# Mixer in a new order, LayerNorm by token half, band matrices from the host: one change to a hybrid decoder kernel

## The reference

```python
u = rms_norm(h, norm_mix_g)
b_a, c_a, h_a, v_b, g_b = split(u @ w_in)                 # five parts of 512 channels
y_a = b_a * causal_dwconv(c_a * h_a, conv_a_w)            # 3 taps
cb  = causal_dwconv(v_b * sigmoid(g_b), conv_b_w) + bias  # 31 taps
y_b = silu(layer_norm(cb, ln_b_g, ln_b_b))                # over 512 channels
h   = h + concat(y_a, y_b) @ w_out
h   = h + cross_attention(rms_norm(h), rms_norm(mem))     # 4 heads
h   = h + relu(rms_norm(h) @ w_up) ** 2 @ w_down          # width 4096
# after both layers: rms_norm(h, final_g)
```

## Time and profile before

| | us |
|---|---|
| median of 3 runs | 3471.89 (3469.18 to 3646.47) |
| the profiled execution | 3468.78 |
| its span, slowest core | 3467.2 |
| spans of all cores | 3442.4 to 3467.2 |
| TensorE busy | 3257.5 (94%) |
| VectorE / ACT / POOL busy | 1762.9 / 1402.1 / 643.7 |

### The profile page before, as it was taken

One profiled execution on the slowest core, in us unless ns is written; L12 is line 12 of the kernel. 1 busy time (PEld: TensorE's weight loads), 2 busy tenths in 40 slices (PEclk: granted clock), 3 DMA queues, 4 the chain that ended last, 5 costly groups with the idle time before them and its releaser, 6 DMA issues.

```text
span 3467.2 us, 50455 instructions; the slowest of 8 cores (3442.4 to 3467.2 us)
## 1 busy us (share of the span) xinstructions
PE 3257.5 (94%) x16080; PEld 1550.2 (45%) x16080; DVE 1762.9 (51%) x2912; ACT 1402.1 (40%) x2627; POOL 643.7 (19%) x884
## 2 busy tenths in 40 slices
PE   2879999999998999989998999999999899999997
PEld 0445444444454444544444444444445444454443
DVE  4846333663357532564347743376335753366433
ACT  3336322463325531464333732256333553146421
POOL 0413001320032100330004200222003210042000
PEclk9989999999999999999999999999999999999999
DMA  7686944544555444535548344344456444453441
GB/s 202 150 187 102 166 73 85 118 91 79 110 167 124 80 78 82 122 79 86 98 94 228 64 80 76 91 113 83 77 117 177 111 80 79 75 127 72 77 80 52
DMA packets 132275, 366.93 MB, mean 106 GB/s; under 512 B 13872, under 2 KB 39728, under 8 KB 132016
## 3 DMA queue, kind: packets, MB, share of 16 engines
q0 software_dynamic: 59648, 213.94, 36.5%
q1 hardware_dynamic: 63152, 145.56, 13.3%
q10 hardware_dynamic: 9216, 4.20, 0.5%
HBM read 521.98 MB, written 34.60 MB: 161 GB/s over the span
## 4 chain that ended last, share of the span: by engine, by line
PE 83%; DVE 4%; issue 4%; DMA 3%; ACT 3%; POOL 1%; SPq 1%; DVEq 0%; ACTq 0%; POOLq 0%
PE ps L450 81%; ACT arena L461 3%; DMA arena<-wts 2%; DVE arena L465 2%; PE ps L906 2%; DVE arena L475 1%; DMA wbf<-arena 1%; SPq L577 1%; POOL arena L465 1%; DVE arena L610 0%; POOL arena L479 0%; POOL arena L470 0%; POOL arena L766 0%; DVE arena L951 0%; SPq L589 0%
## 5 line engine op out<-in xcount | busy, mean ns | idle before, releaser
L450 PE MATMUL ps<-arena 128*128 128x512 bf16 (+2 forms) x15816 | 3182.7, 364 | 126.3 <-ACT arena L461 64.9
L450 PEld LDWEIGHTS ps<-arena 128*128 128x128 bf16 x15816 | 1520.8, 98 | 1785.8 <-issue 175.6
L461 ACT ACTIVATE arena<-arena 128x512 bf16<-128x512 f32 (+3 forms) x1249 | 740.6, 642 | 1265.2 <-DVE arena L465 949.3
L465 DVE TENSOR_TENSOR arena<-arena 128x512 bf16<-128x512 f32 (+3 forms) x1200 | 849.5, 715 | 653.6 <-ACT arena L461 632.2
L465 DVE TENSOR_TENSOR arena<-ps,arena 128x512 f32<-128x512 f32 (+1 forms) x448 | 303.2, 688 | 633.7 <-PE ps L450 594.4
L461 ACT ACTIVATE arena<-ps 128x512 f32<-128x512 f32 (+1 forms) x608 | 361.8, 595 | 623.0 <-PE ps L450 599.2
L416 POOL DMA_DIRECT2D arena<-wts x400 | 214.7, 538 | 1662.6 <-PE ps L450 1621.1
L465 POOL TENSOR_TENSOR arena<-arena 128x512 f32<-128x512 f32 (+1 forms) x144 | 206.7, 1439 | 609.3 <-ACT arena L461 366.0
L461 ACT ACTIVATE arena<-ps,arena 128x256 f32<-128x256 f32 (+2 forms) x441 | 228.6, 533 | 135.9 <-DVE arena L471 72.9
L465 DVE TENSOR_TENSOR arena<-arena,ps 128x512 f32<-128x512 f32 x256 | 172.8, 686 | 141.2 <-PE ps L906 81.6
L475 DVE SCALAR_TENSOR_TENSOR arena<-arena 128x384 f32<-128x384 f32 (+3 forms) x336 | 179.3, 586 | 92.0 <-ACT arena L461 91.5
(11 more groups left out here) (14 smaller groups left out, 96.9 us busy)
## 6 DMA issues: line engine op xcount, KB each, us to landing
arena<-wts POOLq DMA_DIRECT2D x400, 512.0 KB, 5.9
arena<-wbf SPq DMA_DIRECT2D x64, 576.0 KB, 4.0
arena<-wbf SPq DMA_DIRECT2D x64, 512.0 KB, 5.4
arena<-xT SPq DMA_DIRECT2D x32, 512.0 KB, 6.8
outT<-arena SPq DMA_DIRECT2D x8, 2048.0 KB, 7.1
arena<-xT SPq DMA_DIRECT2D x6, 2048.0 KB, 15.6
wbf<-arena SPq DMA_DIRECT2D x16, 576.0 KB, 3.7
arena<-arena SPq DMA_DIRECT2D x128, 64.0 KB, 3.5
```

Of the source, the lines that this page charges most:

```text
L450: ins = e.matmul(ps.ap, lhsT=l_, rhs=r_, start=(first and i == 0), stop=(last and i == n - 1))
L461: return e.activation(**kw)
L465: S.op(eng, lambda e: e.tensor_tensor(out=out.ap, in0=a.ap, in1=b.ap, op=op), reads=[a, b], writes=[out])
```

## The change: what it does

- The mixer's order is gates and values 0, c and h 0, gates and values 1, c and h 1, bands, and then all eight b groups, half 0 first. The products of conv_a are kept in eight buffers instead of four. The list of loads follows.
- LayerNorm's normalising and silu_out are done for token half 0 and then for half 1, each on 128 tokens per phase; all of it on VectorE. The output projection waits for each half by itself (await_ln). out_half takes six output blocks and goes block by block.
- The band matrices come from the host, f32, [16, 128, 2304]. In tile 0 they are cast into the ring by POOL's loads, used there, and stored to wbf by SP from the slot. conv_build and the taps are gone.
- The first loads: vectors, then x on SP and, for two pieces of half 0, on ACT; two weights are ahead of x instead of four.
- Seven PSUM banks rotate, one serves the norms. References of strided tiles carry exact intervals. In the last tile the output is multiplied and stored in pairs of channel blocks.

```diff
@@ next_ps, next_aux @@
-            return psref(rot("ps", range(6)))
+            return psref(rot("ps", range(7)))
 
         def next_aux():
-            return psref(6 + rot("aux", range(2)))
+            return psref(7)
@@ order of the weight loads @@
-                    seq += [w_id(l, C_G + jp), w_id(l, C_V + jp)]
-                seq += [w_id(l, C_C), w_id(l, C_H)]
-                seq += [b_id(l, W_CONV + i) for i in range(8)]
-                seq += [w_id(l, C_B), w_id(l, C_C + 1), w_id(l, C_H + 1), w_id(l, C_B + 1)]
+                    seq += [w_id(l, C_G + jp), w_id(l, C_V + jp), w_id(l, C_C + jp), w_id(l, C_H + jp)]
+                seq += [("c", l * 8 + i) if ti == 0 else b_id(l, W_CONV + i) for i in range(8)]
+                seq += [w_id(l, C_B), w_id(l, C_B + 1)]
@@ ring_pump @@
-                if kind == "f":
-                    S.op("pool", lambda e, o=slot.full[:, 0:2048], s=wts[cid]: e.dma_start(out=o, in_=s),
-                         reads=[h[1].r()] if 4 <= i < RING else [], writes=[slot.r(0, 2048)], dma_sem=sem[f"wc{i % RING}"])
+                if kind != "b":
+                    n, src = (SLOT, bands[cid]) if kind == "c" else (2048, wts[cid])
+                    S.op("pool", lambda e, o=slot.full[:, 0:n], s=src: e.dma_start(out=o, in_=s),
+                         reads=[h[1].r()] if 2 <= i < RING else [], writes=[slot.r(0, n)], dma_sem=sem[f"wc{i % RING}"])
@@ first loads @@
-            S.op("sp", lambda e: e.dma_start(out=h[s].r3(2 * i, 2 * i + 2).ap, in_=xT3[:, 2 * i:2 * i + 2, s * T:(s + 1) * T]),
+            S.op("act" if s == 0 and i % 2 else "sp", lambda e: e.dma_start(out=h[s].r3(2 * i, 2 * i + 2).ap, in_=xT3[:, 2 * i:2 * i + 2, s * T:(s + 1) * T]),
                  writes=[h[s].r3(2 * i, 2 * i + 2)], dma_sem=sem[f"xa{s * 4 + i}"])
 
-        load_x0(0, 0)
+        S.op("sp", lambda e: e.dma_start(out=vec.full, in_=vecs), writes=[vec.r()], dma_sem=sem["misc"])
+        for s in range(NS):
+            for i in range(4):
+                load_x0(s, i)
         S.op("sp", lambda e: e.dma_start(out=cstf.full, in_=cst), writes=[cstf.r()], dma_sem=sem["st0"])
-        S.op("sp", lambda e: e.dma_start(out=tapb.full, in_=taps), writes=[tapb.r()], dma_sem=sem["st1"])
-        S.op("sp", lambda e: e.dma_start(out=vec.full, in_=vecs), writes=[vec.r()], dma_sem=sem["misc"])
-        for i in range(1, 4):
-            load_x0(0, i)
-        for i in range(4):
-            load_x0(1, i)
@@ after the first loads: -conv_build, 16 calls of it @@
-            S.op("dve", lambda e: e.tensor_tensor(out=st3, in0=e3, in1=w3_, op=ALU.mult),
-                 reads=[cstf.r(), tapb.r()], writes=[stage.r()])
-            wb_store(l * NWB_L + W_CONV + i, stage.r())
@@ mixer @@
+            def conv_a(s, j, c, cv):
+                act(cv.r3(0, 4), c.r3(0, 4, 1, TAU + 1), AF.Copy, scale=vcol(wa + 2 * 4 + j), extra_reads=[vref])
+                yield
+                for k, lag in ((1, 1), (0, 2)):
+                    w = vcol(wa + 4 * k + j)
+                    hi, lo = cv.r3(lag, 4), cv.r3(0, lag)
+                    stt("dve", hi, c.r3(0, 4 - lag, 1, TAU + 1), w, hi, ALU.mult, ALU.add, extra_reads=[vref])
+                    stt("dve", lo, c.r3(4 - lag, 4, 0, TAU), w, lo, ALU.mult, ALU.add, extra_reads=[vref])
+                tt("pool", cv.r(), cv.r(), RA[s].r(), ALU.mult)
+
+            def ch_part(jp):
+                sc = ring_get(w_id(l, C_C + jp))
+                sh = ring_get(w_id(l, C_H + jp))
+                for s in range(NS):
+                    for jj in range(2):
+                        j = 2 * jp + jj
+                        c = rot("chb", chb)
+                        hh = chh[l].r(2 * j, 2 * j + 2)
+                        h3 = Ref(hh.ap.unsqueeze(2), "sb", hh.lo, hh.hi)
+                        psc = grp(sc, jj, xg, s)
+                        t = tmp()
+                        tt("dve", t.r(), psc, RB[s].r(), ALU.mult)
+                        copy("pool", c.r3(2, 4, 0, 1), h3)
+                        psh = grp(sh, jj, xg, s)
+                        tt("dve", c.r3(0, 4, 1, TAU + 1), ps4(psh), p4(t), ALU.mult)
+                        copy("pool", h3, c.r3(2, 4, TAU, TAU + 1))
+                        spawn(conv_a(s, j, c, cva[s * 4 + j]))
+                ring_free(2)
+
+            gv_part(0)
+            ch_part(0)
+            gv_part(1)
@@ band matmuls @@
+            ch_part(1)
...
-            ch_part(0)
             for cc in range(8):
                 tick()
-                slot = ring_get(b_id(l, W_CONV + cc))
+                slot = ring_get(("c", l * 8 + cc) if ti == 0 else b_id(l, W_CONV + cc))
+                if ti == 0:
+                    wb_store(l * NWB_L + W_CONV + cc, slot.r())
                 ps = next_ps()
@@ LayerNorm @@
+            def silu_out(a, s):
                 for g in range(4 * a, 4 * a + 4):
-                    act(yb.c(g), cb.c(g), AF.Silu, scale=vcol(vb + V_LNG + g), bias=vcol(vb + V_LNB + g), extra_reads=[vref])
+                    act(yb.c(g, s * TAU, (s + 1) * TAU), cb.c(g, s * TAU, (s + 1) * TAU), AF.Silu, scale=vcol(vb + V_LNG + g),
+                        bias=vcol(vb + V_LNB + g), extra_reads=[vref])
...
-                for a in range(5):
-                    if a < 4:
-                        blk = cb.r3(4 * a, 4 * a + 4)
-                        tt("dve", blk, blk, bc(ln_m), ALU.subtract)
-                        tt("pool" if a % 2 else "dve", blk, blk, bc(ln_v), ALU.mult)
-                    if a > 0:
-                        silu_out(a - 1)
+                for s in range(NS):
+                    blks = [cb.r3(4 * a, 4 * a + 4, s * TAU, (s + 1) * TAU) for a in range(4)]
+                    for a in range(2):
+                        tt("dve", blks[a], blks[a], bc(ln_m, s), ALU.subtract)
                     yield
+                    for a in range(4):
+                        if a < 2:
+                            tt("dve", blks[a + 2], blks[a + 2], bc(ln_m, s), ALU.subtract)
+                        tt("dve", blks[a], blks[a], bc(ln_v, s), ALU.mult)
+                        silu_out(a, s)
+                        yield
+                    ln_done.add(s)
                     yield
                 touch(AF.Ln)
 
+            def await_ln(s):
+                while s not in ln_done:
+                    assert tasks
+                    tasks[:] = [t for t in tasks if step(t)]
+
             spawn(ln_task())
-            b_part(0)
-            ch_part(1)
-            b_part(1)
-            finish_tasks()
-            drain_bg()
+            sb_ = [ring_get(w_id(l, C_B)), ring_get(w_id(l, C_B + 1))]
+            for s in range(NS):
+                for j in range(4):
+                    psb = grp(sb_[j // 2], j % 2, xg, s)
+                    tt("dve", phased(ycat, j, s), ps4(psb), p4(cva[s * 4 + j]), ALU.mult)
+            ring_free(2)
             bgwork()
-
-        def attend(l):
+            return await_ln
@@ attend: out_half, O @@
-                    def emit(e, kh=kh):
-                        ins = None
-                        for k in range(4 * kh, 4 * kh + 4):
-                            for ps, m in zip(pss, ms):
-                                ins = e.matmul(ps.ap, lhsT=wk(ok[m // 2], 256)[:, k, (m % 2) * 128:(m % 2 + 1) * 128],
-                                               rhs=rs[k].ap, start=(k == 0), stop=(k == 7))
-                        return ins
-                    tick()
-                    S.op("pe", emit, reads=[ok[m // 2].r(0, 2048) for m in ms[::2]] + rs[4 * kh:4 * kh + 4], writes=pss)
-                for ps, m in zip(pss, ms):
-                    spawn(resid_task(s, m, ps, vb + V_X, rmo[s]))
+                    if kh:
+                        await_ln(s)
+                    for ps, m in zip(pss, ms):
+                        tick()
+                        w3 = wk(ok[m // 2], 256)
+                        mm(ps, [(w3[:, k, (m % 2) * 128:(m % 2 + 1) * 128], rs[k].ap) for k in range(4 * kh, 4 * kh + 4)],
+                           [ok[m // 2].r(0, 2048)] + rs[4 * kh:4 * kh + 4], first=(kh == 0), last=(kh == 1))
+                        if kh:
+                            spawn(resid_task(s, m, ps, vb + V_X, rmo[s]))
             def O(s, m):
+                await_ln(s)
-            out_half(0, (0, 1, 2, 3))
-            for m in range(4, 8):
+            out_half(0, (0, 1, 2, 3, 4, 5))
+            for m in range(6, 8):
@@ end of the last tile @@
+        def final_last(ti, s):
+            t0 = ti * TT + s * T
+            for c in range(8):
+                stt("dve", h[s].c(c), h[s].c(c), vcol(V_FINAL + c), RC[s].r(), ALU.mult, ALU.mult, extra_reads=[vref])
+                if c % 2:
+                    S.op("sp", lambda e, c=c: e.dma_start(out=outT3[:, c - 1:c + 1, t0:t0 + T], in_=h[s].r3(c - 1, c + 1).ap),
+                         reads=[h[s].r3(c - 1, c + 1)], dma_sem=sem[f"oc{s}{c // 2}"])
```

155 lines of the change are left out of this document (66 added, 89 removed).

## The result

The changed kernel takes 1.0119 of the time of the one before, 95% interval 1.0075 to 1.0162: 41 us slower (0.0119 of 3470), where 17 us faster was forecast. Its profiled execution took 3511.84 us. (In two of its four timed runs, 3666 and 3950 us, one die ran at a lower clock, and the ratios here leave such runs out.) The difference is under 2%, but its sign is clear.

What follows compares the result with a forecast made beforehand. TensorE, busy 94% of the span, was taken to bound the kernel, with DMA deciding the start. From the profiled 3468.8, -38 + 17 + 4 gave 3452; the runs' median, 3.1 higher, made it 3455 us, range 3368 to 3510.

Steps and rivals of the forecast that it cites:

- Part 1: Start up to the first output projection: band builds go and idle DMA time is filled, -38 us.
- Part 2: The other seven mixers: moved groups and ACT's longer chain from LayerNorm to scores, +2.5 us each, +17.
- the three waits: TensorE's short waits in a mixer: about 5 us for half 0, 3 for half 1, 4 for scores; clock loss 1.3.
- Part 3: Small things: single norm bank +3, layer 1 of tile 0 +3, the end -2; sum +4 us.
- the single bank: One PSUM bank for norm sums: at each tile change the second channel sum waits for ACT's read, 1 us x 3.
- The tail: The kernel's end: half 0's multiplies delay half 1's last residual, but the last store is smaller, -2 us.
- (a): In the mixers, ACT's DMA issues cost ACT nothing: -64 us in place of +17, result 3374 us; chance 30%.
- (b): In the mixers, a silu costs by the instruction, 0.52 us for 128 columns: +51 us, result 3489; chance 12%.
- (c): The start gives little: loads come as late as now, only some 12 of 38 us saved, 3481; chance 8%.
- the bound of Part 2, +51: Upper bound for the seven mixers: +7.3 us each, with silus of 0.52 us and half clock.

Runs made afterwards that it cites:

- e4: The kernel before with only the change's start (host bands, first loads); mixer order, LayerNorm, PSUM and tail as before: 0.9895 of the kernel before, 3436 us.
- e2: The changed kernel with the second DMA pair of every silu_out issued by POOL instead of ACT: 0.9898 of the kernel before.
- e5: The changed kernel with POOL issuing silu_out's second DMA pair, and si copies ahead of half 1's store and reload on SP's queue: 0.9884 of the kernel before.
- e1: The changed kernel with half 1's store and reload put behind the si copies on SP's queue at tile changes: 1.0087 of the kernel before.
- e10: The changed kernel with POOL issuing silu_out's second pair, si copies ahead of half 1's store and reload, and bands copied HBM to HBM by POOL: 0.9837 of the kernel before.
- e14: e10 with two PSUM banks for norm sums and six that rotate, as before the change: 0.9817 of the kernel before, 3404 us.

## Why the prediction was wrong

**Part 1 was right: -38 forecast.** The first attention starts 37.2 us earlier: in the chain of waits its matmuls moved from 277.66 to 240.49. By the first MLP 32.9 are left, and the start alone is worth 34 to 36 us (e4). The mechanism is right only in part. The DMA share is 1.06 from 140 us on, as forecast, and in e4 PE does wait for weights up to the output projection. In the changed kernel, however, the last wait there is for ACT's silu blocks (27.65 us), and the chain ahead of it, from 95 to 144 us, is band stores in SP's queue. With ACT free weights are last again, and the same attention starts no earlier: on core 5 at 245.97 us in e2 and 243.87 in e5, and at 244.20 in the changed kernel. So two limits fell within some 2 us of each other, and that the number holds for this kernel is partly luck. The first matmul came at 28.16 us, not at 18 to 25: the first half of x, now on two queues, landed at 23.3, and the norm follows it. It did not matter, since other limits came later.

**Part 2 failed in the step "The other seven mixers: +2.5 us each, +17".** They cost 77.5 us. Two things are in that, and they are not of the same kind.

First, a size. For the mixer that was read, the cycle splits in three. First MLP matmul to first silu: +12.5 measured, +12.45 forecast (13.7 - 1.25). First silu to scores: 37.0, forecast 35.1 (41.3 - 6.2), mostly because a block took 3.2 us and not 3.04. Behind the scores' start +1.7, and that is the clock. The stretches behind the three waits (busy us of each engine, granted clock, DMA share, GB/s), after, and then the last one before:

```profile
1484.00:1490.00 6.00, 3.18 (x10) 1.31 (x11) 0.99 (x2) 3.29 (x8) 0.00 (x0) 0.81 0.64 198
1499.00:1504.00 5.00, 3.61 (x16) 1.48 (x16) 2.93 (x5) 4.99 (x11) 0.00 (x0) 1.00 0.01 3
1508.00:1514.00 6.00, 5.20 (x22) 2.17 (x23) 3.12 (x7) 4.01 (x9) 0.00 (x0) 0.72 0.00 1
```
```profile
1510.00:1517.00 7.00, 7.00 (x37) 3.12 (x36) 4.87 (x11) 5.60 (x13) 1.07 (x1) 1.00 0.26 77
```

A mean of 0.72 is part of the stretch at 1.2 GHz, after the engine had waited 5.69 us, and 6 x 0.28 = 1.7 us, at most, as 0.8 us of the stretch is idle. Behind the wait of 4.53 us it is 0.81, but there ACT's chain is longer anyway; behind the one of 2.19 us the clock stays full. The forecast had 1.3 for the clock at all three waits together. Sum +4.9 against +2.5; in three such mixers 16.8 us instead of 7.5. The mechanism, ACT's order with its DMA issues, was right, and e2 shows its whole size: without those issues the mixer is 11 us shorter, 6 shorter than before.

Second, a step that is not in the prediction: "the other seven" took the layer-1 mixer for all. In the three mixers at a change of tile it is +20.8, +18.6 and +13.9, 53.3 us in place of 10.5 with Part 3's 1 us each. The change moves the si copies eight groups down, past items that SP's queue takes in between: the final store and the reload of half 1. In Part 2 the prediction spoke of ACT's queue only. The timelines of PE show where it went. From the first MLP matmul to LayerNorm's first, with the 13.7 us of moved groups taken off, the three take 13.3, 11.4 and 6.2 us longer than before, where the layer-1 mixer takes 1.1 us less. In that stretch are the waits ahead of the bands (9.55, 6.90 and 6.25 us, in place of 2.42, 2.30 and 5.80 before), the 2.88 us of the single bank, and some 3 us more, of which the clock behind the waits is a part (0.63 from 1030 to 1035 us). Behind LayerNorm's first matmul they lose 7 to 8 us, the layer-1 mixer 6. e1 shows the first item to be the order of copies and reload: without it 7 to 10 us go on core 3, 5 to 7 on the mean of four cores. e2, which leaves this order, gains 15 to 17 us here against 11 in layer 1, since the waits ahead of the bands shrink with it too (to 2.96, 4.34 and 2.23 us); why they do is open.

**Part 3:** layer 1 of tile 0 cost +7.4 (2.5 + 3 forecast), for a reason that was only half seen. It isn't bandwidth alone: SP's queue holds the so copies behind eight stores, and PE waits 20.6 us for them, its longest wait for copies (e5 and e10 show the cause). The tail came out at -1.8 (-2 forecast). The single bank, +3, was the right wait at a third of its size (2.88 us three times, and clock; e14 is without it); in the sum below it stands within the changes of tile.

Sum: -32.9 + 7.4 + 53.3 + 16.8 - 1.8 = +42.8, the difference of the spans. The forecast was -17 against the profiled run; of the 60 us between, the changes of tile are 43, the sizes in layer 1 of tiles 1 to 3 are 9, and the start 5.

**The rivals.** (a), ACT's DMA issues cost ACT nothing, had 30% and is false: behind each issue in the mixer shown above the next activation starts 0.1 us later, never inside it, and taking the issues away gained 77 us. The Trainium skill's rule, page "Advanced Engine Details and Errata", section "Sequencer and Instruction Queues", that other engine instructions can be read and queued while a control instruction runs, doesn't help an activation behind a DMA issue in this trace. POOL's row was the right one to go by. (b), a silu costs by the instruction, is false: 0.41 us for 128 columns, as forecast, with 0.52 for 256. Its result, 3489, is near the truth by accident. (c) is false too.

The range ended at 3510 and the measured run was 3511.5; the bound of Part 2, +51, took the worst of the layer-1 mixer seven times, so it too left out the changes of tile. That the miss of the range is so small says nothing for the mechanism.

## What to carry to other kernels

A chain of short activations and small DMAs is as long as both, if the activations' engine issues the DMAs. The issues belong on the queue whose engine has nothing due at that moment, and which one that is depends on the order: POOL gained 77 us in the new order and lost 24 in the old.

When a change moves groups, list for every queue what is interleaved by step count, in each kind of stage. Reading one mixer in full priced that one to 2.4 us; the three at a change of tile, where a 2 MB reload is issued just ahead of small copies, missed by 43 us. And when a queue seems to hold a copy, look at when its input was ready and how long its transfer took: in tile 0 the queue was the price, at the changes of tile the transfer.

A part that is slower as built may still be right: the order and the halving lose some 78 us as written, and are 20 to 28 us ahead of the old order once their queues are mended.

## What was unexpected of the hardware

- Small SBUF copies (64 KB) landed 8.7 and 13.2 us after their issue, on two different queues, beside a reload of 2 MB, and 2.8 and 3.1 us after it where nothing large ran.
- A copy with a cast from HBM to HBM (0.59 MB written) took 47.36 us in one case beside the MLP's weight loads, with a median of 11.4 us over 16; the same bands into SBUF took 8.1.
- Two cores of one chip, in the same execution, differ by 6 us in one cycle at a change of tile (410.1 and 416.6 us), but by 0.3 to 2.8 in a layer-1 cycle.
